# A decoder layer in fp32 on one core: 24 tokens instead of 16 leave the dense expert products

## The reference

```python
q = (x @ w_pq).reshape(b, s, 8, 2, 128)           # 8 heads, two halves
# top 16 of 128 keys in each half, top 16 of the 256 sums: 16 experts per head and token
a = g * gelu(einsum('chkd,cd->chk', peer_u[idx], x), approximate=False)
ff = einsum('chk,chkd->cd', a, peer_v[idx])        # 128 experts per token
x = layer_norm(alpha * x + ff) * gain3 + bias3
```

## Time and profile before

| | us |
|---|---|
| median of 3 runs | 2296.94 |
| lowest and highest | 2296.12, 2297.95 |
| profiled execution | 2296.87 |
| its span, first to last instruction | 2295.1 |

### The profile page before, as it was taken

How to read it: one execution, slowest core, us unless ns; L and a number is a source line. 1 busy time by engine, 2 the same in 40 slices (tenths; PEclk the granted TensorE clock), 3 DMA queues, 4 the chain that set the end, 5 groups by cost and what they waited for, 6 DMA issues and landing times.

```text
span 2295.1 us, 45914 instructions
## 1 busy us (share of the span) xinstructions
PE 2271.5 (99%) x15939; PEld 2122.4 (92%) x15939; DVE 1711.5 (75%) x2307; ACT 1115.5 (49%) x1477; POOL 635.1 (28%) x442
## 2 busy tenths in 40 slices
PE   9999999999999999999999999999999999999997
PEld 9988899888898899999999999999899998998996
DVE  5444566665744577999999999998688887777767
ACT  4444555653433344544555545554455555454454
POOL 1000100000001026878755667557100000004000
PEclk9999999999999999999999999999999999999999
DMA  9787644466454657788888888888999987778874
GB/s 368 253 279 266 193 154 149 156 215 218 155 183 133 195 159 152 182 198 194 196 196 196 199 193 196 196 197 203 303 326 314 318 311 256 254 268 285 301 231 143
DMA packets 334140, 509.84 MB, mean 222 GB/s; under 512 B 68688, under 2 KB 216400, under 8 KB 326512
## 3 DMA queue, kind: packets, MB, share of 16 engines
q1 hardware_dynamic: 284832, 441.69, 62.6%
q0 software_dynamic: 48528, 66.36, 11.9%
q10 hardware_dynamic: 704, 0.75, 0.1%
HBM read 485.33 MB, written 21.23 MB: 221 GB/s over the span
## 4 chain that ended last, share of the span: by engine, by line
PE 95%; DMA 2%; DVE 2%; ACT 1%; issue 0%; POOL 0%; DVEq 0%; SPq 0%; ACTq 0%
PE ps L781 30%; PE ps L486 19%; PE ps L816 17%; PE ps L489 16%; PE ps L822 9%; DMA v_raw<-in_peer_v_dram 2%; PE ps L700 1%; PE ps L725 1%; PE ps L475 1%; PE ps L522 0%; ACT v_hi L1230 0%; DVE v_lo L1904 0%; PE ps L762 0%; PE ps L616 0%; PE ps L906 0%; DMA region<-in_x_dram 0%
## 5 line engine op out<-in xcount | busy, mean ns | idle before, releaser
L1503 DVE TENSOR_TENSOR split_ring<-weight_ring,split_ring 128x1024 fp32r<-128x1024 f32 x288 | 351.3, 1228 | 310.4 <-ACT split_ring L968 299.2
L1410 POOL DMA_INDIRECT gates_scratch<-sb_gains x256 | 500.2, 1954 | 236.4 <-ACT sb_gains L1143 120.3
L781 PE MATMUL ps<-parts,u_hi 128*128 128x240 f32 x4096 | 498.7, 274 | 0.0
L816 PE MATMUL ps<-e_pair,v_hi 128*128 128x480 f32 x2016 | 479.0, 378 | 2.2 <-ACT v_hi L1230 1.7
L781 PEld LDWEIGHTS ps<-parts,u_hi 128*128 128x128 f32 x4096 | 477.2, 190 | 0.0
L968 ACT ACTIVATE split_ring<-weight_ring 128x1024 fp32r<-128x1024 f32 x288 | 303.0, 1058 | 339.0 <-PE ps L486 212.3
L1904 DVE TENSOR_TENSOR v_lo<-v_raw,v_hi 128x1024 fp32r<-128x1024 f32 x252 | 308.2, 1223 | 170.1 <-ACT v_hi L1230 169.4
L1148 ACT ACTIVATE u_hi<-u_turned 128x1024 fp32r<-128x1024 f32 x256 | 271.9, 1062 | 329.4 <-DVE u_turned L1763 327.7
L486 PE MATMUL ps<-split_ring,parts 128*128 128x512 f32 x1872 | 429.7, 390 | 0.0
L1230 ACT ACTIVATE v_hi<-v_raw 128x1024 fp32r<-128x1024 f32 x252 | 267.3, 1061 | 329.8 <-PE ps L822 264.3
L486 PEld LDWEIGHTS ps<-split_ring,parts 128*128 128x128 f32 x1872 | 350.1, 188 | 72.6 <-issue 0.4
(11 more groups left out here) (252 smaller groups left out, 1138.7 us busy)
## 6 DMA issues: line engine op xcount, KB each, us to landing
u_raw<-in_peer_u_dram SPq DMA_DIRECT2D x1024, 128.0 KB
v_raw<-in_peer_v_dram SPq DMA_DIRECT2D x256, 512.0 KB, 5.4
weight_ring<-in_w_in_dram SPq DMA_DIRECT2D x96, 512.0 KB, 5.0
weight_ring<-in_w_mkv_dram SPq DMA_DIRECT2D x64, 512.0 KB, 3.9
gates_scratch<-temps POOLq DMA_DIRECT2D x16, 1024.0 KB, 7.3
weight_ring<-in_w_o_dram SPq DMA_DIRECT2D x32, 512.0 KB, 4.5
weight_ring<-in_w_mq_dram SPq DMA_DIRECT2D x32, 512.0 KB, 4.6
weight_ring<-in_w_mo_dram SPq DMA_DIRECT2D x32, 512.0 KB, 3.9
```

What stands on the lines that cost most here:

```text
L781: m = nc.tensor.matmul(ps[:, b, 0:ET], u[:, k * P:(k + 1) * P], x2T[n][kk][:, 0:ET], start=not done and kk == 0 and n == 0, stop=done and ...
L816: return nc.tensor.matmul(ps[:, tile, 0:PAIR], v_hi[slot][:, tile * P:(tile + 1) * P], e_pair[e][:, b * PAIR:(b + 1) * PAIR], start=start, ...
L1410: pool.indirect_dma_start(gates_by_one, bass.IndirectOffsetOnAxis(ap=idx_all[:, j:j + 1], axis=0), gate_all[:, j:j + 1], None, compute_op= ...
L1503: nc.vector.tensor_tensor(w_lo[j % SPLIT], raw[j % RAW], w_hi[j % SPLIT].bitcast(F32), ALU.subtract).then_inc(lo_ready, 1)
```

## The change

The last 24 tokens leave the dense products, so `ET` is 232 and a pair 464 columns. The eight more tokens use the layout a second time: a partition holds a sixteenth of such a token's experts, that is eight more lines of U and of V (`LINES` = 48), in columns 16 to 23 of `line_of` and `line_gate`. They have their own rows of x2 (`more_lines`, two tiles of 1024 columns, loaded by 32 transfers of eight 4 KB rows) and their own sum in the same tiles (`more_sum`), folded in four steps of two transfers and added to `x2_back` by two more. DVE's half lines come every 2 half blocks instead of 3, dots from n = 18, sums from n = 132 as before. POOL's queue is ordered anew: 32 more copies of indices and gates; the first gathers wait for `v_used` 9, 13 and 17 instead of 12, 17 and 22; the loads for `more_lines` stand between gathers 2 and 6; the copies of the turned output stand eight at a time between gathers; the loads of x2 stand between the last gathers and no longer wait for `e_lo_ready`.

```diff
-        PICKED = 16
-        GROUPED = P // PICKED
-        ET = T - PICKED
-        LINES = 2 * P * PICKED // P
-        LINE_FROM, SUM_FROM, LINE_STEP = 20, 132, 3
+        PICKED, MORE = 16, 8
+        GROUPED, MORE_GROUPED = P // PICKED, P // MORE
+        ET = T - PICKED - MORE
+        DOTS = PICKED + MORE
+        LINES = 2 * DOTS
+        LINE_FROM, SUM_FROM, LINE_STEP = 18, 132, 2
...
+            for j in range(MORE_GROUPED):
+                to, of = slice(MORE * j, MORE * j + MORE), slice(P - PICKED - MORE, P - PICKED)
+                pool.dma_start(line_of[to, 16:24], pick_of[of, 8 * j:8 * j + 8]).then_inc(pick_landed, 16)
+                pool.dma_start(line_gate[to, 16:24], gate_all[of, P + 8 * j:P + 8 * j + 8]).then_inc(pick_landed, 16)
...
                 if c < 3:
-                    pool.wait_ge(v_used, 5 * c + 12)
+                    pool.wait_ge(v_used, 4 * c + 9)
...
-            for c in range(LINES - 5):
+            for c in range(3):
+                gather(c)
+            for j in range(MORE_GROUPED):
+                for n in range(2):
+                    pool.dma_start(more_lines[n][MORE * j:MORE * j + MORE, :], picked_dram[0:MORE, n * HALF:(n + 1) * HALF])\
+                        .then_inc(x2_lines_landed, 16)
+                if j % 4 == 3:
+                    gather(3 + j // 4)
+            for c in range(7, LINES - 12):
                 gather(c)
             pool.wait_ge(out_turned_ready, 1)
-            for a in range(2):
+            for a in range(4):
                 first_out_rows(a)
-            gather(LINES - 5)
-            for a in range(2, 4):
-                first_out_rows(a)
-            gather(LINES - 4)
+                gather(LINES - 12 + a)
+            for c in range(LINES - 8, LINES - 6):
+                gather(c)
             pool.wait_ge(first_out_landed, 32 * 16)
             pool.dma_start(gain3_b, ln3_g[0].partition_broadcast(P)).then_inc(gb_landed, 16)
-            gather(LINES - 3)
+            gather(LINES - 6)
             pool.dma_start(bias3_b, ln3_b[0].partition_broadcast(P)).then_inc(gb_landed, 16)
-            gather(LINES - 2)
-            load_x2_back(0)
+            for n in range(4):
+                gather(LINES - 5 + n)
+                load_x2_back(n)
             gather(LINES - 1)
-            for n in range(1, 4):
-                pool.wait_ge(e_lo_ready, PAIRS - 26 + 4 * n)
-                load_x2_back(n)
...
+            for n, rows_left in enumerate((64, 32, 16, 8)):
+                if n:
+                    pool.wait_ge(more_folded, 32 * n)
+                for r in more_sum:
+                    pool.dma_start(r[0:rows_left, :], r[rows_left:2 * rows_left, :], accum_op=ALU.add).then_inc(more_folded, 16)
...
+            pool.wait_ge(more_folded, 128)
+            for n in range(2):
+                pool.dma_start(x2_back[P - PICKED - MORE:P - PICKED, 1, n * HALF:(n + 1) * HALF], more_sum[n][0:MORE, :],
+                               accum_op=ALU.add).then_inc(more_folded, 16)
...
-                m = nc.vector.tensor_tensor_reduce(lines[c % 3][:, part], lines[c % 3][:, part], x2_lines[:, part],
+                of = x2_lines[:, part] if c < PICKED else more_lines[q][:, :]
+                m = nc.vector.tensor_tensor_reduce(lines[c % 3][:, part], lines[c % 3][:, part], of,
...
+                to = line_sum[:, part] if c < PICKED else more_sum[q][:, :]
+                if c in (0, PICKED):
...
                     dve.wait_ge(line_folded, 64)
+                    dve.wait_ge(more_folded, 160)
```

More of the change, by code:

```diff
@@ L221, in layer_program @@
         pick_of = keysT[:, P:2 * P].bitcast(U32)
[L222 to L224 removed]
+        line_of, line_gate = rope_cs[:, 0:DOTS].bitcast(U32), rope_cs[:, DOTS:2 * DOTS]
+        line_half = dfg[:, 0:2 * DOTS]
+        line_dot, line_act = dfg[:, 2 * DOTS:3 * DOTS], dfg[:, 3 * DOTS:4 * DOTS]
         cos2 = rope_cs[:, :].rearrange("p (t c) -> p t c", t=NT)[:, :, 0:ROT]
@@ L1414, in _ @@
                 to, of = slice(PICKED * j, PICKED * j + PICKED), slice(P - PICKED, P)
-                pool.dma_start(line_of[to], pick_of[of, 16 * j:16 * j + 16]).then_inc(pick_landed, 16)
-                pool.dma_start(line_gate[to], gate_all[of, P + 16 * j:P + 16 * j + 16]).then_inc(pick_landed, 16)
+                pool.dma_start(line_of[to, 0:16], pick_of[of, 16 * j:16 * j + 16]).then_inc(pick_landed, 16)
+                pool.dma_start(line_gate[to, 0:16], gate_all[of, P + 16 * j:P + 16 * j + 16]).then_inc(pick_landed, 16)
+            for j in range(MORE_GROUPED):
+                to, of = slice(MORE * j, MORE * j + MORE), slice(P - PICKED - MORE, P - PICKED)
+                pool.dma_start(line_of[to, 16:24], pick_of[of, 8 * j:8 * j + 8]).then_inc(pick_landed, 16)
+                pool.dma_start(line_gate[to, 16:24], gate_all[of, P + 8 * j:P + 8 * j + 8]).then_inc(pick_landed, 16)
             for j in range(GROUPED):
                 pool.wait_ge(v_used, 4 + j)
-                pool.dma_start(x2_lines[PICKED * j:PICKED * j + PICKED, :], picked_dram).then_inc(x2_lines_landed, 16)
-            pool.wait_ge(pick_landed, 2 * GROUPED * 16)
+                pool.dma_start(x2_lines[PICKED * j:PICKED * j + PICKED, :], picked_dram[MORE:]).then_inc(x2_lines_landed, 16)
+            pool.wait_ge(pick_landed, 2 * (GROUPED + MORE_GROUPED) * 16)
             def gather(c):
                 if c < 3:
-                    pool.wait_ge(v_used, 5 * c + 12)
+                    pool.wait_ge(v_used, 4 * c + 9)
                 else:
@@ L1428, in gather @@
                 carry_wait()
-                k = c % PICKED
-                pool.indirect_dma_start(lines[c % 3], None, (peer_u if c < PICKED else peer_v)[0],
+                k = c % DOTS
+                pool.indirect_dma_start(lines[c % 3], None, (peer_u if c < DOTS else peer_v)[0],
                                         bass.IndirectOffsetOnAxis(ap=line_of[:, k:k + 1], axis=0)).then_inc(line_landed[c % 3], 16)
@@ L1923, in dot_half @@
                     dve.wait_ge(x2_lines_landed, GROUPED * 16)
+                if n == 2 * PICKED:
+                    dve.wait_ge(x2_lines_landed, (GROUPED + 2 * MORE_GROUPED) * 16)
                 if q == 0:
@@ L1934, in add_half @@
                 c, q = divmod(n, 2)
-                slot = (LINES // 2 + c) % 3
+                slot = (DOTS + c) % 3
                 if q == 0:
-                    dve.wait_ge(line_landed[slot], (LINES // 2 + c) // 3 * 16 + 16)
+                    dve.wait_ge(line_landed[slot], (DOTS + c) // 3 * 16 + 16)
                     if c == 0:
@@ L1940, in add_half @@
                     else:
-                        dve.wait_ge(line_used, LINES // 2 + 1 + c)
+                        dve.wait_ge(line_used, DOTS + 1 + c)
                 part = slice(q * HALF, (q + 1) * HALF)
-                if c == 0:
-                    m = nc.vector.tensor_scalar(line_sum[:, part], lines[slot][:, part], line_dot[:, 0:1], None, ALU.mult)
-                else:
-                    m = nc.vector.scalar_tensor_tensor(out=line_sum[:, part], in0=lines[slot][:, part],
-                                                       scalar=line_dot[:, c:c + 1], in1=line_sum[:, part],
-                                                       op0=ALU.mult, op1=ALU.add)
+                to = line_sum[:, part] if c < PICKED else more_sum[q][:, :]
+                if c in (0, PICKED):
+                    m = nc.vector.tensor_scalar(to, lines[slot][:, part], line_dot[:, c:c + 1], None, ALU.mult)
+                else:
+                    m = nc.vector.scalar_tensor_tensor(out=to, in0=lines[slot][:, part], scalar=line_dot[:, c:c + 1],
+                                                       in1=to, op0=ALU.mult, op1=ALU.add)
                 if q == 1:
@@ L1954, in line_work @@
                 for first, work in ((LINE_FROM, dot_half), (SUM_FROM, add_half)):
-                    if first <= n < first + LINES * LINE_STEP and (n - first) % LINE_STEP == 0:
+                    if first <= n < first + 2 * DOTS * LINE_STEP and (n - first) % LINE_STEP == 0:
                         work((n - first) // LINE_STEP)
```

8 lines of the change are left out of this document (5 added, 3 removed).

## The result

The changed kernel takes 2302.1 us (median of 17 runs, 2298.6 to 2310.9) against 2296.9 before (17 runs, 2295.1 to 2299.2). The ratio is 1.0028, 95% interval 1.0021 to 1.0035: slower by 0.28%, where I had forecast 0.24% faster. The spread of the runs has grown too, from 4 to 12 us. The profiled execution took 2301.78 us with a span of 2300.0.

The account below looks back on a forecast made before the run. The prediction took TensorE as the bound, busy for 99% of the span, with DMA close behind in the last stage. Terms -12.5 + 1.5 + 3 + 1.5 + 1 = -5.5 us gave 2291.4 from 2296.9, range 2279 to 2303.

Parts of the forecast that it names:

- V hi: Last stage's 2016 wide products, 480 to 464 columns: 11.2 to 13.4 us less, 12.5 taken.
- V lo: Last stage's 2016 narrow products, 240 to 232 columns: 6.7 us less by the line, nothing with a floor; 0 taken.
- U: Middle stage's 6144 products, 240 to 232 columns: bounds 0 and 5 us gain, set by VectorE's idle time; 0 taken.
- Rival 1: No floor in U and V: matmuls follow their columns, U gains 5 us before DVE stops it; 2278.8 us, chance 0.17.
- VectorE: First pass of V: 32 more half lines, 4.56 us of DVE work per two half blocks against 5.14 of PE, hidden.
- POOL's copies: 32 more index and gate copies before the x2 loads, some 15 us, fit POOL's 15.2 us free: 0.
- The steady part of the dots: V's half blocks 18 to 113: DMA must move 352 GB/s; bounds 0 and 5 us lost, 1.5 taken.
- Rival 2: DMA becomes the bound in the dots' stretch; at 330 GB/s 16 us lost instead of 1.5: 2306 us, chance 0.20.
- The second x2 rows: 32 loads of eight 4 KB rows, 1 MB, between gathers 2 and 6: bounds 0 and 6 us lost, 3 taken.
- Rival 3: Gather 36, fold chain and x2 rows land late, each at upper bound, some 5 us more: 2296.4, no change, chance 0.18.
- Second pass: After the output turn, gather 36's line up to 2 us late and loads among gathers: 1.5 us added, bounds 0 and 5.
- The folds: End of V: fold chain of 52.1 us against 51.4 available; 1 us lost, bounds 0 and 6.

Follow-up runs that it names:

- e1: Kernel before with the dense products 8 columns narrower and nothing in their place (eight tokens wrong): 2286.9 us, ratio 0.9959.
- e11: Kernel before with U's products and V's narrow products over 128 token columns instead of 240: 2301.3 us (one run).
- e12: e1 plus only the 32 loads of the second x2 rows, read by nobody; lines and first gathers as before: 2299.6 us.
- e3: Changed kernel without the 32 loads of the second x2 rows; the added dots use the first set (wrong results): 2292.2 us.
- e17: e12 with the second x2 rows in sixteen loads of sixteen partitions instead of 32 of eight, same place: 2292.5 us.
- e5: Changed kernel with the 32 second-row loads in eight lots of four before gathers 7 to 14, instead of four lots of eight: 2299.4 us.
- e7: Changed kernel with the second x2 rows loaded by two transfers of 128 partitions instead of 32 of eight: 2298.6 us.
- e15: Changed kernel with the second rows in two 128-partition loads before gathers 11 and 13, and gather 36 before the turn: 2294.6 us.
- e4: Changed kernel with the first three gathers waiting for half blocks 12, 17 and 22 as before: 2302.9 us.
- e6: Changed kernel with both sets of x2 rows loaded from different rows of U instead of one small DRAM scratch (dots wrong): 2306.2 us.
- e9: Changed kernel with gather 36 issued before POOL waits for the turned output, later copy lots each followed by a gather: 2300.2 us.

## Why the prediction was wrong

**V hi, V lo, U: right in sum.** 12.5 us were forecast and the starts give 12.3, but the parts made up for each other: V hi gave 2016 x 5.1 ns = 10.3 us, below its bounds of 11.2 to 13.4, and V lo gave 2.0 where I had nothing. That the sum fits is partly luck. e1 has 10.0 us by the medians. The zero for U was no matter of VectorE's little idle time: U's products keep 111.66 to 111.67 ns at 128 (e11), 232 and 240 columns. Rival 1 is dead. That the floor is the weight load was not tried. The Trainium skill (TensorE: Matmul & The Clock Gate, LDWEIGHTS) prices a weight load at P / 1.2 ns, 106.7 ns for 128 columns. The floor of 111.67 ns in these traces lies 5 ns above that.

**VectorE, POOL's copies: right.** The first load of x2 rows went out at 1614.2 us against 1613.4 before.

**The steady part of the dots: right.** 350 GB/s at a share of 0.96, with 0.18 us of idle PE where I had 1.5 us. Rival 2 had the right side (slower) and the right resource, and the wrong place: not a line every four half blocks over 96 of them, but the first 100 us.

**The second x2 rows: the step that failed.** I wrote "Bounds 0 and 6; I take 3", from the megabyte of the first set. Alone they cost 12.6 us (e12 against e1), and the whole kernel without them is 10 us faster (e3). The row that I used was of sixteen 8 KB rows to a transfer, one transfer to a half block, before the gathers had begun; these are 32 transfers of eight 4 KB rows in lots of eight between gathers, and the form is worth up to 7 us (e17). I also counted only the bytes not moved, not that PE can come back from a long gap at the lower clock and lose another 1.4 to 2.9 us, as it did in these profiles after every gap of 2.7 us and more in stage V.

**Rival 3: its sum was wrong.** "Each at their upper bound, some 5 us more" does not follow from the bounds that I had set: 6 for the rows, 5 for the second pass and 6 for the folds, in place of 3, 1.5 and 1, are 11.5 us more, 2302.9. Added up rightly, this rival forecast a slower kernel, and not "no change"; its chance belonged in part to "slower". That 2302.9 lies so near the 2302.1 measured is luck, since the rows alone cost twice their bound.

**Second pass: mis-sized by little.** 1.5 us were forecast, the profile has 2.9 us more gaps there in total. The wait that I named came, 3.2 us where I had up to 2: DVE stands for line 36, as its timeline in the changed kernel shows.

```profile
2086.75 1.28 DVE L1971 SCALAR_TENSOR_TENSOR region<-region,dfg,region 128x1024 f32<-128x1024 f32 x1 [3.18 <-DMA region<-in_peer_v_dram,rope_cs]
```

**The folds: right to a microsecond.** 1 us was forecast. In this profile the residual that waits for them ran at 2258.1 us with no wait before it, by the same timeline:

```profile
2258.11 1.22 DVE L2003 SCALAR_TENSOR_TENSOR y_out<-x_back,y_out 128x1024 f32<-128x1024 f32 x1
```

But in the profiles of e5, e7 and e15 DVE did wait for the last fold, by 0.7, 2.6 and 1.1 us. Of e7, what waited, for what, us in total, times, longest:

```profile
DVE y_out L2002 <- DMA x_back<-more_lines: 2.6, 1, 2.6
```

The chain just fits in some executions and just fails to in others.

The parts other than the rows cost e3 - e1 = 5.2 us, with several us of noise, where I had 1.5 + 1.5 + 1 = 4. With 12.6 for the rows the pieces make 2286.9 + 12.6 + 5.2 = 2304.7, near the 2302.1 measured.

**Open.** The early first gathers make the gap near 1643 us; what they cost in time is not shown, since e4 has none of it and is no faster. PE idles 3.9 to 4.1 us there in the four profiles in which the second rows follow gather 2 or 3 (after, e6, e7, e9) and 1.8 to 2.1 us in the three in which they come later or not at all (e3, e5, e15), though the first of those loads is issued at 1655.8 us in the changed kernel, behind the gap. That is not explained. The changed kernel's runs spread over 12 us, and no run says why. What it is in the form that costs is open too. The expectations speak of half of the DMA engines, or of a row for each of the sixteen; no trace here tells the DMA engines apart, so neither was tested.

## What to carry to other kernels

Before narrowing a matmul, look at the start-to-start distance of products with fewer columns in the same trace: where it does not fall, narrower products give nothing, however many there are. In a stretch where the DMA share is above 0.9, price a small load by a run of its own, not by its bytes: one megabyte cost 5.6 to 12.6 us by its form and density, against 3 us of transfer time. Before moving a load to the queue of an engine that feeds the matmuls, count what its issuing holds up: sixteen loads held ACT for 6.9 us. And try a gain of 12 us alone first: it shows at once how much the work that pays for it may cost.

## What the runs showed of the hardware

- fp32r products of 128, 232 and 240 columns with a weight load each: 111.66 to 111.67 ns from start to start in a uniform stream. In V's mix eight products of 128 columns took 0.84 us instead of 0.90, and the eight of 480 beside them 1.78 instead of 1.72: the sum did not move.
- fp32r products of 256 and 512 columns take 120.0 and 226.7 ns, 13.3 ns more than their columns at 2.4 GHz each. At 240 columns that sum would be 113.3, and 111.67 is measured, so the line does not go on down to there.
- In the changed kernel PE came back from 4.0 us of idle time at 387 ns for a product of 464 columns, and the same again at 1678 us after 3.2 us. Over stage V of all profiles, with a gap taken as the distance of two starts beyond the usual one, those of 2.7 us and more were followed by slow products that cost 1.4 to 2.9 us more; of those between 2.0 and 2.5 us some were (2.04 us in e5, with a granted clock of 0.70 in 2120.4 to 2126) and some were not (2.30 us in e9, clock 1.00 in 1638 to 1644); gaps under 2.0 us cost at most 0.5 us more.
- Reading rows of U instead of a 192 KB scratch made the small loads no cheaper (e6).
